# The compress stage of a hybrid attention layer: turns of the next half set between the products of the half at hand

## What is computed

```python
def compress(rows, pe, w1, w2):
    b, l, h, d = rows.shape
    nc = l // CMP_BLOCK
    blocks = rows.reshape(b, nc, CMP_BLOCK, h, d) + pe[None, None, :, None, :]
    flat = blocks.transpose(0, 1, 3, 2, 4).reshape(b, nc, h, CMP_BLOCK * d)
    return jax.nn.silu(flat @ w1) @ w2
...
    def past_rows(pool):
        return pool[page_table].reshape(b, past, NSA_KV_HEADS, HEAD_DIM)

    nc = total // CMP_BLOCK
    kc_all = jnp.concatenate([past_rows(cache_cmp_k), k_cmp], axis=1)[:, :nc * CMP_BLOCK]
    vc_all = jnp.concatenate([past_rows(cache_cmp_v), v_cmp], axis=1)[:, :nc * CMP_BLOCK]
    ck = rms_norm(compress(kc_all, cmp_pe_k, cmp_w1_k, cmp_w2_k), k_norm_g)
    cv = compress(vc_all, cmp_pe_v, cmp_w1_v, cmp_w2_v)
```

## Time and profile before

| | us |
|---|---|
| median of 3 runs | 1064.61 (1063.58 to 1066.42) |
| profiled execution, its own time | 1061.0 |
| its span, first to last instruction | 1059.3 |
| compress stage, first transpose to last small product | 519.8 to 596.5 |
| TensorE busy, of the span | 950.8 (90%) |
| VectorE busy | 492.7 (47%) |

### The profile page before, as it was taken

One profiled execution on the slowest core, in us unless ns is written; L12 is line 12 of the kernel. 1 busy time (PEld: TensorE's weight loads), 2 busy tenths in 40 slices (PEclk: granted clock), 3 DMA queues, 4 the chain that ended last, 5 costly groups with the idle time before them and its releaser, 6 DMA issues. The chain is left out here.

```text
span 1059.3 us, 15611 instructions
## 1 busy us (share of the span) xinstructions
PE 950.8 (90%) x5223; PEld 714.6 (67%) x5223; DVE 492.7 (47%) x1068; ACT 308.0 (29%) x694; POOL 183.9 (17%) x209
## 2 busy tenths in 40 slices
PE   4799999999999989999777688999999993699998
PEld 2387869997868777878576675566666652466775
DVE  4724242346244555440335157776675752463522
ACT  4501012223132333141000155655554631310100
POOL 2211222333102211100150001110010014222000
PEclk9999999999999999999899669999999996799999
DMA  5350802000611023113492140000000036875531
GB/s 179 111 139 0 241 18 82 1 1 1 260 63 45 1 80 96 55 40 112 98 207 61 46 133 21 21 21 21 1 21 20 1 115 159 240 234 164 180 105 44
DMA packets 89837, 91.12 MB, mean 86 GB/s; under 512 B 27885, under 2 KB 67997, under 8 KB 89397
## 3 DMA queue, kind: packets, MB, share of 16 engines
q1 hardware_dynamic: 70530, 74.42, 23.1%
q10 hardware_dynamic: 16508, 8.78, 3.2%
q0 software_dynamic: 2720, 6.94, 2.5%
HBM read 75.51 MB, written 23.49 MB: 93 GB/s over the span
## 5 line engine op out<-in xcount | busy, mean ns | idle before, releaser
L827 PE MATMUL ps<-w_high,x_high 128*128 128x512 f32 (+3 forms) x576 | 225.0, 391 | 9.9 <-PEq L131 7.3
L829 PE MATMUL ps<-w_high,x_low 128*128 128x512 f32 (+3 forms) x576 | 221.0, 384 | 0.0
L828 PE MATMUL ps<-w_low,x_high 128*128 128x512 f32 (+3 forms) x576 | 220.9, 384 | 0.0
L827 PEld LDWEIGHTS ps<-w_high,x_high 128*128 128x128 f32 (+1 forms) x576 | 103.1, 179 | 37.9 <-issue 10.0
L829 PEld LDWEIGHTS ps<-w_high,x_low 128*128 128x128 f32 (+1 forms) x576 | 103.0, 179 | 28.1
L828 PEld LDWEIGHTS ps<-w_low,x_high 128*128 128x128 f32 (+1 forms) x576 | 103.3, 179 | 26.5
L1550 PE MATMUL ps<-k_high,q_stack 128*128 128x512 f32 (+3 forms) x192 | 77.3, 406 | 18.5 <-DVE a_stats L1443 12.9
L491 POOL TENSOR_TENSOR stats<-stats,small 128x8 f32<-128x8 f32 (+3 forms) x35 | 40.7, 1164 | 226.4 <-DVE stats L706 171.1
L1550 PEld LDWEIGHTS ps<-k_high,q_stack 128*128 128x128 f32 x192 | 38.3, 199 | 59.9 <-DVE a_stats L1443 28.9
L1592 PE MATMUL ps<-weights_turned,v_nat 128*64 128x512 f32 x264 | 71.6, 623 | 0.0
L1551 PE MATMUL ps<-k_low,q_stack 128*128 128x512 f32 (+3 forms) x192 | 66.6, 354 | 0.0
(11 more groups left out here) (302 smaller groups left out, 1510.3 us busy)
## 6 DMA issues: line engine op xcount, KB each, us to landing
w_raw<-in_w_in SPq DMA_DIRECT2D x56, 256.0 KB, 4.5
tmp_skew<-tmp_table SPq DMA_DIRECT2D x8, 576.0 KB
x_tile<-in_x_prompt SPq DMA_DIRECT2D x8, 512.0 KB, 5.3
y_rows_in<-tmp_y SPq DMA_DIRECT2D x8, 512.0 KB, 4.9
x_rows<-in_x_prompt SPq DMA_DIRECT2D x8, 512.0 KB, 4.8
out_y_prompt<-out_rows SPq DMA_DIRECT2D x8, 512.0 KB, 5.5
keys_raw<-in_cache_slc_k SPq DMA_DIRECT2D x46, 64.0 KB, 2.4
tmp_y<-stage SPq DMA_DIRECT2D x8, 256.0 KB
```

The lines of the kernel that those rows point to most:

```text
L827: nc.tensor.matmul(out, s.xh[:, k, rows], s.wh[:, k, 0:w], start=(k == 0), stop=False)
L828: nc.tensor.matmul(out, s.xh[:, k, rows], s.wl[:, k, 0:w], start=False, stop=False)
L829: ins = nc.tensor.matmul(out, s.xl[:, k, rows], s.wh[:, k, 0:w], start=False, stop=(k == KT - 1))
```

## The change

TensorE's half turns of the next four sequences no longer stand in a block of their own. Only the first eight half turns do. After that, a product's 32 matmuls are written in groups of four, and ahead of each group stands one half turn of the next half (`turn_half(then + i // 4)`), so a product carries the turns of the half after it. The last product has none. `second(0)` now stands behind the third product and its turns, that is ahead of the fourth product.

SyncE issues its half of the key weights ahead of all pages, ScalarE too; both halves of the value weights are now ScalarE's, behind its pages of u = 7. SyncE keeps pages 0 to 2, ScalarE has 3 and 4, GpSimd 5 to 7.

On VectorE `key_means` stands behind all moves. The prompt's copy for the values, which overwrites columns that the keys' second product reads, waits for that product.

```diff
--- before.py
+++ after.py
@@ -971,7 +971,7 @@
 
 SAMPLE = [0, 4, 1, 5, 2, 6, 3, 7]
 SLOTS, FIRST = 8, 4
-SP_PAGES, ACT_PAGES, POOL_PAGES = range(0, 3), range(3, 6), range(6, 8)
+SP_PAGES, ACT_PAGES, POOL_PAGES = range(0, 3), range(3, 5), range(5, 8)
 
 
 def persistent_compressed(nc, s):
@@ -1043,11 +1043,9 @@
 
         @block.sync
         def _(sp):
-            load_pages(sp, FIRST, SP_PAGES, raw_in)
             load_w1(sp, 0, 0)
-            for u in range(FIRST + 1, SLOTS):
+            for u in range(FIRST, SLOTS):
                 load_pages(sp, u, SP_PAGES, raw_in)
-            load_w1(sp, 1, 0)
             sp.wait_ge(zeroed, 1)
             for kv in range(2):
                 for half in range(2):
@@ -1085,11 +1083,11 @@
         @block.scalar
         def _(act):
             own = Chain(act, a_steps)
-            load_pages(act, FIRST, ACT_PAGES, raw_in)
             load_w1(act, 0, 1)
-            for u in range(FIRST + 1, SLOTS):
+            for u in range(FIRST, SLOTS):
                 load_pages(act, u, ACT_PAGES, raw_in)
-            load_w1(act, 1, 1)
+            for half in range(2):
+                load_w1(act, 1, half)
             for u in range(SLOTS, 2 * B):
                 load_pages(act, u, ACT_PAGES, raw_in)
             for kv in range(2):
@@ -1117,6 +1115,8 @@
             own = Chain(dve, v_steps)
 
             def keep_prompt(kv):
+                if kv == 1:
+                    dve.wait_ge(first_out, 2)
                 nc.vector.tensor_copy(kcs[:, :, NBS:NBS + NBP], s.kct[:, kv, :].rearrange("p (i n) -> p i n", i=CB)).then_inc(prompt_kept, 1)
 
             def evacuate(u):
@@ -1159,8 +1159,7 @@
                 if u % B == 4:
                     keep_prompt(u // B)
                 evacuate(u)
-                if u == B + 5:
-                    key_means()
+            key_means()
             key_norms()
             dve.wait_ge(key_high, 1)
             own.step(nc.vector.tensor_copy(s.cks[:], s.ps[:, KEYS, 0:2 * P]))
@@ -1169,22 +1168,25 @@
 
         @block.tensor
         def _(pe):
-            def turn(u):
+            def landed(u):
                 if u < FIRST:
                     pe.wait_ge(s.c_first[u], 16 * PAGES)
                 else:
                     loads = u // SLOTS + (1 if u % SLOTS >= FIRST else 0)
                     pe.wait_ge(raw_in[u % SLOTS], 16 * (PAGES - len(POOL_PAGES)) * loads)
                     pe.wait_ge(raw_in_pool[u % SLOTS], 16 * len(POOL_PAGES) * loads)
-                for half in range(2):
-                    i = 2 * u + half
-                    if i >= 3:
-                        pe.wait_ge(evacuated, i - 2)
-                    for j in range(4):
-                        last = nc.tensor.transpose(s.ps[:, i % 3, P * j:P * j + P], raw(u)[:, 4 * half + j, :], s.ident[:])
-                    last.then_inc(turned, 1)
-
-            def first(kv, half):
+
+            def turn_half(i):
+                u, half = i // 2, i % 2
+                if half == 0:
+                    landed(u)
+                if i >= 3:
+                    pe.wait_ge(evacuated, i - 2)
+                for j in range(4):
+                    last = nc.tensor.transpose(s.ps[:, i % 3, P * j:P * j + P], raw(u)[:, 4 * half + j, :], s.ident[:])
+                last.then_inc(turned, 1)
+
+            def first(kv, half, then):
 
                 cols = slice(0, NBS // 2) if half == 0 else slice(NBS // 2, NBS + NBP)
                 if half == 0:
@@ -1197,6 +1199,8 @@
                     pe.wait_ge(prompt_kept, kv + 1)
                 pe.wait_ge(evacuated, 2 * B * kv + B * (half + 1))
                 for i in range(CB):
+                    if then and i % 4 == 0:
+                        turn_half(then + i // 4)
                     last = nc.tensor.matmul(s.ps[:, 4 + kv, cols], w1[:, kv, i, :], kcs[:, i, cols], start=(i == 0), stop=(i == CB - 1))
                 last.then_inc(first_out, 1)
 
@@ -1218,11 +1222,12 @@
                     last = nc.tensor.transpose(s.ps[:, KEYS, at:at + NBP], dup[0:NBP, h, :, :].rearrange("p a d -> p (a d)"), s.ident[0:NBP, 0:NBP])
                 last.then_inc(key_turned, 1)
 
+            for i in range(B):
+                turn_half(i)
             for kv in range(2):
                 for half in range(2):
-                    for b in range(4):
-                        turn(B * kv + 4 * half + b)
-                    first(kv, half)
+                    done = 2 * B * kv + B * (half + 1)
+                    first(kv, half, done if done < 4 * B else None)
                     if kv == 1 and half == 0:
                         second(0)
             turn_keys()
```

## The result

| | before | changed |
|---|---|---|
| median, 4 runs each | 1064.09 us (1062.58 to 1066.42) | 1050.28 us (1048.57 to 1051.13) |
| profiled execution, its own time | 1061.0 | 1050.63 |
| its span | 1059.3 | 1048.7 |
| first turn to last product's end | 74.97 | 61.96 |

The ratio is 0.9874, with a 95% interval of 0.9851 to 0.9898: 13.8 us faster by the medians. The prediction was 1051.8 us, minus 12.8, so its direction and size held.

A forecast was written before the change was run, and what follows sets the result against it. TensorE and VectorE were taken to bound the stage by turns. Last product's start, minus 10.4, and clock, minus 2.4, took 1061.0 to 1048.2; plus 3.6 for the median, 1051.8 us (forecast 1049.5 to 1054.5, range 1048.0 to 1058.0).

The forecast's parts named there:

- Unit prices: TensorE at full clock: a slot of four turns and four matmuls takes 1.34 us, or 1.54 with 160 columns.
- Start of the first product: Weights issued earlier, so VectorE's last move ends the wait: start about 531.6 in place of 532.64, 1.0 us gained.
- GpSimd is the pace: GpSimd issues three pages a sequence, 1.15 us each; last at about 566.9, landed 569.6; about 5 us lost.
- The stall ahead of the second product: TensorE waits 3 us or more there for GpSimd's third page of the ninth sequence, at no further cost.
- No gap over 0.8 us: After the second product's stall, TensorE idles before turns for up to 0.8 us once a sequence.
- Key norms, cost 0: Means behind VectorE's moves, powers and norms, 5 us together, lie under the 8.8 us last product; cost 0.
- The last product: Its 32 matmuls run at full clock: 8.77 us in place of 11.16 with the small products; minus 2.4.
- SyncE and ScalarE's queues: SyncE's last page out at about 564, ScalarE through earlier; cost 0, at most 2 us against 1 of slack.
- Rival 1: GpSimd does not pace; TensorE alone ends the stage at 576.8: minus 18 us, 1046.6; 6 in 100.
- Rival 2: Half the gain: last product opens at low clock, end pages land in 5.5 us; minus 7.6, 1057; 17 in 100.
- Rival 3: Turns between products keep TensorE at 1.2 GHz; stage 14 us slower, 1079; 6 in 100.
- Rival 4: The next stage gives the gain back behind the barrier, no change: 1064; 4 in 100.

The follow-up runs named there:

- e3: Kernel before with only the key weights issued ahead of the fifth sequence's pages on SyncE and ScalarE; 1063.01 us, ratio 0.9994.
- e10: Kernel before, unchanged, traced a second time; 1062.23 us, one run.
- e11: Kernel before, unchanged, traced a third time; 1063.82 us, one run.
- e4: Changed kernel with pages split 3, 1, 4, so GpSimd issues four of each sequence and ScalarE one; 1063.52 us, ratio 0.9997.
- e5: Changed kernel with 32 pages for each of the three queues, shares varying by sequence; 1045.03 us, ratio 0.9836.
- e1: Changed kernel with the turns put back in blocks behind each product, new loads kept; 1058.87 us, ratio 0.9964.
- e8: Changed kernel, nothing altered, run and traced again; 1049.17 us, ratio 0.9877.

## Why the prediction was right, step by step

- **Unit prices: right.** 1.33 and 1.53 us a slot were measured for 1.34 and 1.54. Across all 24 slots, the time from 531.64 to the small products at 572.06 holds 5.2 us more than the plain pitches and the low clock of the first two slots; take that off and TensorE alone would end at 566.8, for the predicted 567.1. Seams cost nothing.
- **Start of the first product: right.** Its first turn starts at 531.64 for 531.6, and e3 shows the step alone, 1.0 us against the trace that the prediction used. Against e10 and e11 it is 1.7 and 1.9. The low clock at its beginning cost 1.7 us (slots of 2.49 and 1.84 in place of 1.33), as forecast.
- **GpSimd is the pace: right, and tested.** Last page 566.65 for 566.9, landing 2.6 for 2.7, the end of the turns and their products 572.06 for 572.3, and 5.2 us of waits for "about 5". e4 moved the end by its pitch, and e5 made the stage 3.2 us shorter.
- **The stall ahead of the second product: mis-sized.** It was to be "3 us or more" and was 1.18. The bounds were fair in the text: pages landing at 545.2 to 548.0, TensorE ready from 542.3 to 544. TensorE was ready at 544.1 and the pages were there at 545.3 (GpSimd's third went out at 542.24), the early end of the one and the late end of the other; their difference was taken in place of the nearest pair. It cost nothing, as said, since the end hangs on GpSimd.
- **"No gap over 0.8 us" later: slightly short.** It was 0.81 and then 1.16 ahead of the last sequence. Of the signs of being wrong one shows faintly: a move of VectorE's ends the wait ahead of the third product, of 0.19 us.
- **Key norms, cost 0: right as a cost, wrong as a term.** Nothing on TensorE waits for the means in the changed kernel, as said. But the sum gives minus 10.4 to the last product's start without a term for what the means cost before, and in e1, without any turn between products, the way to the last product is 2.0 us shorter and the last product has the full clock. I read the 1.27 us wait ahead of the last turns only as a cause of the low clock; VectorE's rows in that block would have told that the means stand in it. The total was not touched, since it was taken from where the changed kernel's pages let it end.
- **The last product: right**, 8.80 us at 1.00 for 8.77.
- **SyncE and ScalarE's queues: right.** SyncE's last page went out 44.3 us after the first turn, at 564, as forecast.
- **From the profiled execution to the median.** The sum was laid on one trace that was 3.6 and 2.8 us short in this stage against its two repeats and 3.7 short in attention against one of them. The changed kernel's stage was forecast well; that the difference from this one trace, 12.8, lies so near the 13.8 of the medians is in part luck. The stage in e10 to the stage in e8 is minus 17.1, and by one pair of traces alone the gain could have been read as anything from 13 to 17.
- **TensorE's lead over before:** a slip of the sum. 582.7 less 567.1 and less 565.4 is 15.6 and 17.3, not 15 and 16.5; nothing rests on it.
- **Rival 1, TensorE alone, 18 us:** not what this split gives. Yet its price was right: 74.97 less 1.7 for the low clock at the start, less 55.2, is 18.1. e5 is on the way there.
- **Rival 2, the late pages and low clock of the end:** neither came (2.6 us landing, clock 1.00).
- **Rival 3, turns keep the clock low:** fell. The row that decides is a window of the first product, with turns between its matmuls throughout (columns as in the windows above):

```profile
536.00:538.00 2.00, 2.00 (x21) 2.00 (x20) 1.43 (x3) 0.00 (x0) 1.94 (x2) 1.00 1.28 191
```

  The clock stayed at 1.00 from there to the last product's end. The Trainium skill, TensorE: Matmul & The Clock Gate, Part 4: PE-mode transpose, says that transposes do not bring the full clock. Four of them to every four matmuls did not keep it low here. Nor did transposes alone: in the same trace the first block of turns is TensorE's only work from 519.78 on, the clock is 0.50 at first, and it rises while these turns run.

```profile
527.00:528.00 1.00, 1.00 (x6) 0.76 (x5) 1.00 (x3) 0.00 (x0) 0.54 (x1) 0.50 1.18 292
528.00:529.00 1.00, 0.95 (x7) 0.66 (x6) 1.00 (x2) 0.00 (x0) 0.54 (x1) 0.83 1.15 288
```

  At 529 to 530 it is 1.00. For these fp32 transposes the measurement decides against the rule.
- **Rival 4, given back behind the barrier:** the traces of before spread by as much as was missing, so nothing of it is shown.

## What to carry to other kernels

Where two engines take turns being the bound, because one fills a buffer for the other in blocks, write the next block's small steps between the steps of the present one. Then count what each DMA queue must issue by its pitch per transfer and balance the counts, since a queue of register loads and transfers can bind with the DMA engines a third loaded. Look at what a moved side step (here the means) does to the waits of the block it leaves, not only of the place it goes to. And before a difference of 3 us between two traces is called the change's, take a second trace of the old kernel.

## What the runs showed of the hardware that was not expected

- The same wait did not give the same clock. The second product, behind 2.04 or 2.05 us of idle time in each, stands with 8.93 us in the first trace of before and with 10.61 in e1, e3, e10 and e11; the third, behind 2.05 to 2.07, with 8.74 in e10 and with 7.38 in the four others. The last product took 11.1 to 11.4 us in all four traces that have 1.27 us of idle time ahead of the last turns and 2.04 to 2.06 behind them (before, e3, e10, e11), and 8.8 in all nine others. What tells the cases of the second and third product apart is open.
- The attention stage of unchanged code took 292.4, 292.5 and 296.1 us in three executions of one kernel. What stands ahead of the changed stage varies as well: its first turn starts between 519.15 and 523.30 us in the thirteen traces. No cause was looked for.
- A page of 64 KB costs GpSimd 1.14 or 1.15 us of issue in nearly all rows (a few steps took 1.43 to 1.47), and SyncE 1.14: with 96 pages on three queues, 32 each, that is 37 us, in a stage whose TensorE work is 55.
